# A third level buffer, later level steps, and six indexer dot products in flight with a projection's passes among them

## The chip, the cores and the metric

The kernel runs on one core of one Trainium2 chip. The metric is the device time of one execution in microseconds (us), lower is better. Before the change the median of three runs is 1547.05 us (1544.74 to 1548.55). The engines: TensorE (PE in the rows) multiplies matrices; PEld is its loading of weights; VectorE (DVE), ScalarE (ACT) and GpSimd (POOL) work elementwise; SyncE (SP) issues most transfers. Each engine runs its own list in order, and the lists meet at semaphores.

## The reference, cut to what matters

Two decoder layers, each of three parts: a mixer with three groups of heads, cross-attention into a fixed memory, and a mixture of gated experts. The change touches only the mixer:

```python
h = rms_norm(x, norm_mix[l]);  z = h @ w_in[l]          # 512 tokens, width 1024
# indexer: 8 heads of 64; every query keeps 128 causal keys
dots = einsum('bthd,bsd->bths', q_idx, k_idx) * 64**-0.5
score = einsum('bths,bth->bts', relu(dots), w_idx)       # causal mask, then top-k
# sparse attention: 6 heads of 64 on the kept keys, softmax, values
# gated linear attention (GLA): 4 heads, key width 48, value width 96
attn[t,s] = sum_d q[t,d] * k[s,d] * exp(b[t,d] - b[s,d]) # b = running sum of log decays
o = attn @ v + (q * exp(b)) @ state
# conformer branch: ca * sigmoid(cg), causal depthwise convolution with 31 taps, layer norm, silu
x = x + concat(o_gla, o_dsa, o_conv) @ w_out[l]
```

## The kernel before

Everything stays on one core, four tiles of 128 tokens. Projections that need full precision in the "split" form (`split_project`) run as three passes (head times head, rest times head, head times rest) per 128 rows of weights, so a projection of eight parts has 24 passes; the others (`project`) run one float32 product per part, which the trace shows as two records. A projection n goes into PSUM bank n % 2 and ScalarE evicts it (`evacuate`).

**Dot products.** After the index projections (`JOBS` "ik" and "iq") TensorE makes 32 dot products (`DOTS`: 4 tiles of tokens by 8 heads; 128, 256, 384, 512 columns wide), L806 to L811, each over 64 of the 128 rows, even heads in the upper half and odd ones in the lower. They go to the four banks 4 to 7. ScalarE takes the relu of each into one of four `relu` tiles (L1000 to L1005), VectorE weights and adds it to the scores `sel` (L1164 to L1172). A dot product waits for the relu four before it, a relu for the sum four before it. After the 32 dots comes the first query projection, `project(AFTER_IDX)` (L818), then five more projections of queries and keys with their norm sums, and four of values. Meanwhile VectorE does the top-k rounds (`selection`) and at the end six normalisations (L1193, semaphore `normed`), for which the first logits wait.

**Steps.** Then come 24 steps n = (tile i, head h) of attention. In each, TensorE turns the softmaxed row (`turn`, L843; it waits for `normalise(n)` on ScalarE, L1040), every second step makes the values of two heads (`values`, L854) and the logits of two more (`logits`, L834), and fills the rest with parts of other projections and GLA products, spread by a pace over `LAST_FILLED` = 22 steps (`work_of`, L534 to L547). On ScalarE a step is normalise(n), exps(n+1), the level's exponentials, `turned(n)` (eviction of the turned row), and at the end the evictions of the projections that ended in this step. On VectorE it is the reciprocal of the row sum (L1208), `masked(n+1)` (L1203), level work, top-k rounds of the last tile, convolution taps (`conv_tap`, L1217 to L1220; 62 of them, spread by `taps_spread` from the step after the gate "cg" is done up to step 21), and a level difference.

**Levels.** GLA's decayed products inside a tile are made in seven levels (`HALVES` 1 to 64). For level v: VectorE subtracts (`differences`, L1229), ScalarE takes exponentials (`level_decays`), VectorE multiplies the queries (`level_queries`, L1237), GpSimd the keys (`level_keys`, L1352), TensorE multiplies (`level_products`, L783), and VectorE or ScalarE merges the result into `AT`. Level v starts in step LEV0+v; the two `lev` buffers alternate, and a difference waits until the products two levels before are made. The product without decay (`diagonals`) uses buffer 1. By the pace before, LEV0 is 5, the gate's sigmoid runs in step 10 and the taps start in step 11.

The parts of `work_of` per step, before: 8, 8, 8, 7, 7, 5, 5, 4, 5, 5, 6, 6, 6, 6, 7, 7, 6, 6, 5, 4, 5, 3, 0, 0. The first four projections end exactly at the ends of steps 0, 1 and 2 and in step 4; heads 0 and 1 of GLA's output stand first in step 19, heads 2 and 3 end step 21.

## Time and profile before

| | |
|---|---|
| median of three runs | 1547.05 us (1544.74 to 1548.55) |
| profiled execution | 1550.28 us, of which 1548.4 us is the span of the trace |
| TensorE busy | 1435.3 us, 93% |
| VectorE busy | 1157.7 us, 75% |
| ScalarE busy | 908.0 us, 59% |
| GpSimd busy | 556.9 us, 36% |
| mean granted TensorE clock | 0.974 of full |
| dot products, layer 0 | 55.9 to 75.1 us |
| attention steps, layer 0 and 1 | 128.65 to 300.0 and 893.3 to 1064.6 us |

How to read it: times are us from the start of the span, unless marked ns. An instruction row gives start, length, engine, line of the kernel, operation and shapes; "x7" merges seven instructions in a row, and the square bracket is the idle time of the engine before it and what ended it. The granted clock is TensorE's, as a share of 2.4 GHz; 0.50 is its other level, 1.2 GHz.

### The profile page before, as it was taken

The page shows a single profiled execution, that of the slowest core. Times are in us where ns is not written, and L with a number is a line of the kernel's source. Part 1 is how long each engine was busy: PE and PEld are TensorE (multiplying, and loading weights), DVE is VectorE, ACT ScalarE, POOL GpSimd, SP SyncE. Part 2 cuts the span into 40 slices and gives each one's busy share as a digit, 9 for nine tenths or more (in the row PEclk, how much of TensorE's full clock was granted, in tenths as well). Part 3 has the DMA queues.
Part 4 walks back from the last instruction along what each step waited for, and adds up shares of the span by engine and source line. Part 5 has one row for each costly group of instructions (what it writes and reads, how often), then busy time and mean ns, then how long its engine had stood idle before and what let it go on. Part 6 is the DMA issues. An engine that isn't in the chain of part 4 may idle for free.

```text
span 1548.4 us, 20214 instructions
## 1 busy us (share of the span) xinstructions
PE 1435.3 (93%) x6710; PEld 1034.6 (67%) x6710; DVE 1157.7 (75%) x1658; ACT 908.0 (59%) x1346; POOL 556.9 (36%) x240
## 2 busy tenths in 40 slices
PE   7998989899899999999799989888988999999995
PEld 4686554557577888877556855544675778887773
DVE  4696579433469999999858955893334899999996
ACT  5643353553548787888475523546435587887881
POOL 2342332060004665553542413220600066555544
PEclk9999999999989999999999999999999899999998
DMA  6241601310428999999651421014131499999995
GB/s 222 92 109 41 216 1 55 137 57 11 153 109 288 397 398 399 398 398 399 232 190 42 109 75 74 1 55 144 49 107 57 154 342 399 399 399 398 398 397 177
DMA packets 151483, 312.72 MB, mean 202 GB/s; under 512 B 33158, under 2 KB 46380, under 8 KB 151228
## 3 DMA queue, kind: packets, MB, share of 16 engines
q1 hardware_dynamic: 140300, 271.39, 48.5%
q0 software_dynamic: 6624, 24.12, 4.2%
q10 hardware_dynamic: 4496, 16.40, 2.6%
q8 instruction: 36, 0.59, 0.2%
q14 instruction: 27, 0.22, 0.0%
HBM read 287.76 MB, written 29.50 MB: 205 GB/s over the span
## 4 chain that ended last, share of the span: by engine, by line
PE 50%; DVE 20%; DMA 15%; ACT 7%; issue 6%; POOL 1%; DVEq 1%; POOLq 0%; SPq 0%; ACTq 0%
PE ps L703 12%; DMA arena<-in_w_down 9%; PE ps L721 6%; DVE rest_w_down L1417 6%; PE ps L1494 4%; DMA arena<-in_w_gate 4%; DVE rest_w_up L1417 3%; DVE rest_w_gate L1417 3%; PE ps L1516 3%; DVE xg_rest L1430 2%; PE ps L724 2%; PE ps L810 2%; PE ps L1610 2%; PE ps L783 2%; ACT head_w_down L1412 1%
## 5 line engine op out<-in xcount | busy, mean ns | idle before, releaser
L2080 POOL TENSOR_TENSOR rest_w_down<-arena,head_w_down 128x2048 fp32r<-128x2048 f32 x30 | 191.3, 6377 | 191.5 <-ACT head_w_down L1412 191.5
L1417 DVE TENSOR_TENSOR rest_w_down<-arena,head_w_down 128x2048 fp32r<-128x2048 f32 x30 | 151.8, 5059 | 13.6 <-ACT head_w_down L1412 13.6
L1417 DVE TENSOR_TENSOR rest_w_gate<-arena,head_w_gate 128x2048 fp32r<-128x2048 f32 x64 | 145.8, 2279 | 0.1
L1417 DVE TENSOR_TENSOR rest_w_up<-arena,head_w_up 128x2048 fp32r<-128x2048 f32 x64 | 143.4, 2280 | 0.1
L1412 ACT ACTIVATE head_w_down<-arena 128x2048 fp32r<-128x2048 f32 x60 | 115.1, 1926 | 37.8 <-DMA arena<-in_w_down 37.4
L1412 ACT ACTIVATE head_w_gate<-arena 128x2048 fp32r<-128x2048 f32 x60 | 114.8, 1919 | 38.1 <-DMA arena<-in_w_gate 38.0
L1412 ACT ACTIVATE head_w_up<-arena 128x2048 fp32r<-128x2048 f32 x64 | 121.9, 1943 | 9.4 <-DMA arena<-in_w_up 9.4
L1401 PE MATMUL ps<-head_w_gate,xg_head 128*128 128x512 f32 x256 | 104.2, 407 | 4.4 <-DVE xg_rest L1430 3.5
L721 PE MATMUL ps<-hT,arena 128*128 128x512 f32 x224 | 106.4, 606 | 0.0
L1391 PE MATMUL ps<-head_w_down,he_head 128*128 128x512 f32 x240 | 99.6, 415 | 6.6 <-DVE rest_w_down L1417 4.1
L1403 PE MATMUL ps<-head_w_gate,xg_rest 128*128 128x512 f32 x256 | 100.2, 392 | 0.0
L1402 PE MATMUL ps<-rest_w_gate,xg_head 128*128 128x512 f32 x256 | 99.9, 390 | 0.0
L1401 PE MATMUL ps<-head_w_up,xg_head 128*128 128x512 f32 x256 | 99.8, 390 | 0.0
L1403 PE MATMUL ps<-head_w_up,xg_rest 128*128 128x512 f32 x256 | 99.7, 389 | 0.0
L1402 PE MATMUL ps<-rest_w_up,xg_head 128*128 128x512 f32 x256 | 99.6, 389 | 0.0
L1220 DVE SCALAR_TENSOR_TENSOR mixr<-arena,cf,mixr 128x512 f32<-128x512 f32 x120 | 94.4, 787 | 4.3
L1393 PE MATMUL ps<-head_w_down,he_rest 128*128 128x512 f32 x240 | 94.2, 392 | 0.0
L1392 PE MATMUL ps<-rest_w_down,he_head 128*128 128x512 f32 x240 | 93.6, 390 | 0.0
L2027 POOL DMA_INDIRECT xg<-hrows,slot_tok x2 | 4.9, 2437 | 240.8 <-DVE slot_tok L1998 240.8
L703 PE MATMUL ps<-hT_head,w_rest 128*128 128x512 f32 x224 | 89.0, 397 | 0.0
L2073 POOL DMA_INDIRECT xg<-hrows,idx x28 | 76.4, 2727 | 21.0 <-POOL idx L2086 21.0
L951 ACT ACTIVATE arena<-ps 128x512 f32<-128x512 f32 (+1 forms) x34 | 18.8, 558 | 110.0 <-PE ps L721 52.7
(366 smaller groups left out, 3545.4 us busy)
## 6 DMA issues: line engine op xcount, KB each, us to landing
arena<-in_w_gate SPq DMA_DIRECT2D x64, 1024.0 KB, 10.2
arena<-in_w_up SPq DMA_DIRECT2D x64, 1024.0 KB, 11.2
arena<-in_w_down SPq DMA_DIRECT2D x64, 1024.0 KB, 10.4
arena<-in_w_in SPq DMA_DIRECT2D x10, 1536.0 KB, 6.7
yrows<-yb ACTq DMA_DIRECT2D x30, 512.0 KB, 6.3
arena<-in_w_in SPq DMA_DIRECT2D x4, 2048.0 KB, 8.6
x<-in_x SPq DMA_DIRECT2D x8, 512.0 KB, 14.0
arena<-in_w_in SPq DMA_DIRECT2D x16, 256.0 KB, 4.9
```

Source lines behind the costliest of these rows:

```text
L703: last = nc.tensor.matmul(o, lhs, rhs, start=(c == 0 and a == 0), stop=(c == KD - 1 and a == 2))
L721: last = nc.tensor.matmul(ps[n % 2][0:width, :], w[:, c, col:col + width], hT[:, c, :], start=(c == 0), stop=(c == KD - 1))
L1220: do(nc.vector.scalar_tensor_tensor(o, cin[:, i, j:j + S], convw[:, i, j:j + 1], o, ALU.mult, ALU.add))
L1391: nc.tensor.matmul(out, ah, bh, start=(c == 0), stop=False)
L1392: nc.tensor.matmul(out, ah, bl, start=False, stop=False)
L1393: last = nc.tensor.matmul(out, al, bh, start=False, stop=(c == n - 1))
L1401: nc.tensor.matmul(ps[q][:, :], xh[:, c, :], wh[q][:, c, :], start=(c == 0), stop=False)
L1402: nc.tensor.matmul(ps[q][:, :], xh[:, c, :], wl[q][:, c, :], start=False, stop=False)
L1403: last = nc.tensor.matmul(ps[q][:, :], xl[:, c, :], wh[q][:, c, :], start=False, stop=(c == KD - 1))
L1412: nc.scalar.activation(wh[q][:, part(q, j), :], raw[q][:, part(q, j), :], ACT.Copy).then_inc(s_head[q], 1)
L1417: nc.vector.tensor_tensor(wl[q][:, c, :], raw[q][:, c, :], wh[q][:, c, :].bitcast(F32), ALU.subtract).then_inc(s_split[q], 1)
L2080: nc.gpsimd.tensor_tensor(wl[2][:, c, :], raw[2][:, c, :], wh[2][:, c, :].bitcast(F32), ALU.subtract)\
```

## The change

- The dots go to six banks (2 to 7) and six relu tiles (`RELUS`, `DOT_BANK`); the waits are on the relu and the sum six before.
- `project(AFTER_IDX)` after the dots is gone; its 24 passes are issued two at a time after every second dot from dot 9 on (`first_query_passes`).
- A third `lev` buffer, in the place of the second and third part of `gr`; `differences(v)` waits for the products three levels before; `level_queries(v)` comes a step later; the eviction of those parts of `gr` waits for all level products. `diagonals` uses the third buffer.
- ScalarE evicts the turned row before the level's exponentials.
- TensorE's order in a step: turn, logits, values, all parts, then diagonals and level products.
- The pace is set in two pieces: the projections of GLA's queries and keys and of the convolution over steps 0 to 7, the rest over steps 8 to 21. The parts per step become 10, 10, 9, 9, 7, 7, 6, 7, 5, 5, 5, 6, 4, 5, 6, 4, 6, 4, 4, 3, 5, 2, 0, 0. LEV0 becomes 4, the gate's sigmoid falls in step 7, the taps are spread from step 8 on (the first in step 10), heads 0 and 1 end step 18.

```diff
+RELUS = 6
-            lev = [view(mixg[:, :, :].rearrange("p h s -> p (h s)"), 1024 * i, 2, S) for i in range(2)]
+            lev = [view(mixg[:, :, :].rearrange("p h s -> p (h s)"), 1024 * i, 2, S) for i in range(2)] + [view(arena, up + 5120, 2, S)]
-            relu = view(scratch, 0, 4, S)
+            relu = view(scratch, 0, RELUS, S)
+            def DOT_BANK(n):
+                return 2 + n % RELUS
-            LAST_FILLED, FIRST_O = 22, 16
+            GATED, LAST_FILLED, FIRST_O = 8, 22, 16
+            def filler(names, steps):
+                return sum(LENGTH[JOBS[n][4]] for n, c in parts if JOBS[n][4] in names) + sum(attention(n) for n in steps)
-            total = sum(LENGTH[JOBS[n][4]] for n, c in parts) + sum(attention(n) for n in range(LAST_FILLED))
+            first, then = range(GATED), range(GATED, LAST_FILLED)
+            paces = [filler(("gq", "gk", "ca", "cg"), first) / len(first), filler(("gv", "kt", "gr", "upd", "o"), then) / len(then)]
-                pace += total / LAST_FILLED
+                pace += paces[n >= GATED]
+                def first_query_passes(start, end):
+                    if start == 0:
+                        pe.wait_ge(sN["proj_out"], AFTER_IDX - 1)
+                        pe.wait_ge(sN["heads_in"], 7)
+                        pe.wait_ge(sN["rests_in"], 4)
+                    wh, wl, at = w_head[0], w_rest[k_of(SPLIT[0])], slice(0, P)
+                    for m in range(start, end):
+                        c, a = m // 3, m % 3
+                        lhs, rhs = ((wh[:, c, at], hT_head[:, c, :]), (wl[:, c, at], hT_head[:, c, :]), (wh[:, c, at], hT_rest[:, c, :]))[a]
+                        last = nc.tensor.matmul(ps[AFTER_IDX % 2], lhs, rhs, start=(m == 0), stop=(m == 3 * KD - 1))
+                    if end == 3 * KD:
+                        last.then_inc(sN["proj_done"], 1)
                 for n, (i, h) in enumerate(DOTS):
-                    if n >= 4:
-                        pe.wait_ge(sN["relu_done"], n - 3)
+                    if n >= RELUS:
+                        pe.wait_ge(sN["relu_done"], n - RELUS + 1)
...
+                    if i and n % 2:
+                        at = n - IH - 1
+                        first_query_passes(at, at + 2)
-                project(AFTER_IDX)
...
                     turn(n)
+                    if n % 2 == 0 and n + 2 < NS:
+                        logits(n + 2)
+                        logits(n + 3)
                     if n % 2 == 0 and n:
                         values(n - 2)
-                    for job, c in work_of[n][:2]:
+                    for job, c in work_of[n]:
                         work(job, c)
...
-                    if n % 2 == 0 and n + 2 < NS:
-                        logits(n + 2)
-                        logits(n + 3)
-                    for job, c in work_of[n][2:]:
-                        work(job, c)
...
+                    if name == "gr" and i:
+                        act.wait_ge(sN["lev_mm"], NLEV + 1)
...
+                    turned(n)
                     if 0 <= n - LEV0 - 1 < NLEV:
                         level_decays(n - LEV0 - 1)
-                    turned(n)
...
-                    if v >= 1:
-                        dve.wait_ge(sN["lev_mm"], v)
+                    if v >= 2:
+                        dve.wait_ge(sN["lev_mm"], v - 1)
...
-                    if 0 <= n - LEV0 - 1 < NLEV:
-                        level_queries(n - LEV0 - 1)
+                    if 0 <= n - LEV0 - 2 < NLEV:
+                        level_queries(n - LEV0 - 2)
```

## Rows read from the trace of the kernel before

**Rows 1.** Sums of stretches: stretch, us, then each engine's busy us, clock, transfers.

```profile
56.80:75.10 18.30, 18.26 (x75) 11.34 (x76) 17.00 (x32) 15.51 (x32) 1.17 (x3) 1.00 0.24 84
...
191.70:288.30 96.60, 87.20 (x490) 50.33 (x490) 81.43 (x124) 45.87 (x97) 23.51 (x21) 0.98 0.06 23
...
956.40:1053.00 96.60, 87.19 (x490) 50.37 (x489) 81.42 (x125) 45.95 (x97) 23.88 (x21) 0.98 0.06 23
```

**Rows 2.** Waits of VectorE, 56.8 to 125.9: total us, times, longest.

```profile
DVE sel L1169 <- ACT scratch L1004: 6.8, 1, 6.8
```

**Rows 3.** Chain of waits, start of the first query projection.

```profile
70.92 11.13 PE ps L703 x48
```

**Rows 4.** Time line of VectorE: last dots added up, six normalisations.

```profile
69.61 5.47 DVE L1171 SCALAR_TENSOR_TENSOR sel<-scratch,iw,sel 128x512 f32<-128x512 f32 x7
...
120.97 4.67 DVE L1193 SCALAR_TENSOR_TENSOR scratch<-scratch,cf,ps 128x512 f32<-128x512 f32 x6
```

**Rows 5.** Time line of TensorE: first logits, first turned row.

```profile
126.47 0.49 PE L834 MATMUL ps<-scratch 64*128 64x128 f32 x4 [0.67 <-ACT scratch L951]
...
128.65 0.33 PE L843 MATMUL ps<-cf,scratch 128*128 128x128 f32 x1 [1.69 <-ACT scratch L1040]
```

**Rows 6.** Instructions by line and shape, both layers: dots of 512 columns.

```profile
L810 PE MATMUL ps<-sq,mixg 64*128 64x512 f32 x32 | 11.6, 641 | 0.0
```

**Rows 7.** Sums of two short stretches, for the granted clock.

```profile
130.00:132.00 2.00, 2.00 (x8) 1.04 (x6) 1.60 (x4) 0.00 (x0) 0.00 (x0) 0.50 0.88 323
...
270.00:272.00 2.00, 1.55 (x14) 1.55 (x15) 1.89 (x4) 1.70 (x4) 0.00 (x0) 1.00 0.00 0
```

**Rows 8.** Waits of TensorE, 128.6 to 288.3.

```profile
PE ps L843 <- ACT scratch L1040: 14.8, 12, 2.3
...
PE ps L783 <- ACT arena L1050: 0.7, 1, 0.7
...
PE ps L735 <- ACT arena L951: 0.3, 1, 0.3
```

**Rows 9.** Time line of TensorE: gaps before steps 1, 12, 19; half clock behind.

```profile
137.71 0.33 PE L843 MATMUL ps<-cf,scratch 128*128 128x128 f32 x1 [0.98 <-ACT scratch L1040]
...
216.76 0.55 PE L843 MATMUL ps<-cf,scratch 128*128 128x128 f32 x3 [2.35 <-ACT scratch L1040]
...
217.83 2.72 PE L724 MATMUL ps<-arena,hT 128*128 128x384 f32 x4
...
223.57 2.85 PE L724 MATMUL ps<-arena,hT 128*128 128x384 f32 x8
...
270.45 0.66 PE L843 MATMUL ps<-cf,scratch 128*128 128x128 f32 x4 [1.68 <-ACT scratch L1040]
```

**Rows 10.** Time line of ScalarE: table load for the sigmoid, copies of head 1.

```profile
203.43 1.28 ACT L954 ACT_TABLE_LOAD   x1
...
274.20 1.78 ACT L932 ACTIVATE mixg<-ps 32x512 f32<-32x512 f32 x3 [0.94 <-PE ps L758]
```

**Rows 11.** Waits of VectorE, 191.7 to 288.3.

```profile
DVE mixg L1229 <- PE ps L783: 4.8, 2, 2.9
...
DVE scratch L1203 <- PE ps L834: 4.2, 3, 2.5
```

**Rows 12.** Chain of waits at the end of the steps.

```profile
292.59 0.66 PE ps L843 x4
...
300.01 6.21 PE ps L903 x14
```

**Rows 13.** Time line of VectorE: difference, decays to the end, taps.

```profile
160.99 1.23 DVE L1229 TENSOR_TENSOR mixg<-arena 128x1024 f32<-128x1024 f32 x1
...
210.72 2.17 DVE L1258 TENSOR_TENSOR arena<-arena 128x1024 f32<-128x1024 f32 x1
...
239.32 5.48 DVE L1220 SCALAR_TENSOR_TENSOR mixr<-arena,cf,mixr 128x512 f32<-128x512 f32 x7
...
245.58 6.20 DVE L1220 SCALAR_TENSOR_TENSOR mixr<-arena,cf,mixr 128x512 f32<-128x512 f32 x7
```

More of the change, by code:

```diff
@@ L582, in vector_us @@
                 us += 1.5 if 0 <= n - LEV0 - 3 < BY_BLOCKS else 0.0
-                us += 0.8 if 0 <= n - LEV0 - 1 < NLEV else 0.0
+                us += 0.8 if 0 <= n - LEV0 - 2 < NLEV else 0.0
                 us += 1.3 if 0 <= n - LEV0 < NLEV else 0.0
@@ L766, in diagonals @@
                         for i in range(2):
-                            last = nc.tensor.matmul(ps[2][:, 4 * c + 2 * i:4 * c + 2 * i + 2], lev[1][:, i, P * c:P * c + P], gated,
+                            last = nc.tensor.matmul(ps[2][:, 4 * c + 2 * i:4 * c + 2 * i + 2], lev[2][:, i, P * c:P * c + P], gated,
                                                     start=True, stop=True)
@@ L1001, in _ @@
                     act.wait_ge(sN["dots_done"], n + 1)
-                    if n >= 4:
-                        act.wait_ge(sN["relu_used"], n - 3)
-                    nc.scalar.activation(relu[:, n % 4, 0:P * (i + 1)], ps[4 + n % 4][:, 0:P * (i + 1)], ACT.Relu,
+                    if n >= RELUS:
+                        act.wait_ge(sN["relu_used"], n - RELUS + 1)
+                    nc.scalar.activation(relu[:, n % RELUS, 0:P * (i + 1)], ps[DOT_BANK(n)][:, 0:P * (i + 1)], ACT.Relu,
                                          scale=ID ** -0.5).then_inc(sN["relu_done"], 1)
@@ L1069, in level_decays @@
                     act.wait_ge(sN["lev_d"], v + 1)
-                    d = halves(lev[v % 2], half)
+                    d = halves(lev[v % 3], half)
                     nc.scalar.activation(d[:, :, half:], d[:, :, half:], ACT.Exp)
@@ L1166, in _ @@
                     dve.wait_ge(sN["relu_done"], n + 1)
-                    r, w = relu[:, n % 4, 0:P * (i + 1)], iw[:, i, h:h + 1]
+                    r, w = relu[:, n % RELUS, 0:P * (i + 1)], iw[:, i, h:h + 1]
                     if h == 0:
@@ L1225, in differences @@
                         dve.wait_ge(sN["proj_out"], done("gk"))
-                    if v >= 1:
-                        dve.wait_ge(sN["lev_mm"], v)
+                    if v >= 2:
+                        dve.wait_ge(sN["lev_mm"], v - 1)
                     bv = halves(b, half)
-                    do(nc.vector.tensor_tensor(halves(lev[v % 2], half), bv, bv[:, :, half - 1:half].to_broadcast([P, 2 * S // (2 * half), 2 * half]),
+                    do(nc.vector.tensor_tensor(halves(lev[v % 3], half), bv, bv[:, :, half - 1:half].to_broadcast([P, 2 * S // (2 * half), 2 * half]),
                                                ALU.subtract), "lev_d")
@@ L1235, in level_queries @@
                     dve.wait_ge(sN["lev_e"], v + 1)
-                    d = halves(lev[v % 2], half)[:, :, half:]
+                    d = halves(lev[v % 3], half)[:, :, half:]
                     do(nc.vector.tensor_tensor(d, halves(gq, half)[:, :, half:], d, ALU.mult), "lev_q")
@@ L1350, in level_keys @@
                     gp.wait_ge(sN["lev_e"], v + 1)
-                    d = halves(lev[v % 2], half)[:, :, :half]
+                    d = halves(lev[v % 3], half)[:, :, :half]
                     do(nc.gpsimd.tensor_tensor(d, halves(gk, half)[:, :, :half], d, ALU.mult), "lev_k")
@@ L1367, in _ @@
                         do(nc.gpsimd.memset(AT, 0.0), "at_zero")
-                        do(nc.gpsimd.tensor_tensor(lev[1], gq, gk, ALU.mult), "lev_k")
+                        do(nc.gpsimd.tensor_tensor(lev[2], gq, gk, ALU.mult), "lev_k")
                     if 0 <= n - LEV0 - 3 < NLEV:
```

4 lines of the change are left out of this document (2 added, 2 removed).

## The prediction

> **What bounds the kernel now.** I read the sums of stretches first, then who waits for whom in them, then the time lines of single steps. A layer has two stretches that the change touches: the dot products of the indexer (56.8 to 75.1 us) with the top-k rounds and projections behind them, and the 24 attention steps (128.6 to 300 us). In the first, VectorE is the chain: 17.00 us of work in 18.30 [rows 1], and from 56.8 to 125.9 it waits for nothing after the first dot product [rows 2]. TensorE has slack there: its last dots end at 70.92 us and the first query projection (24 passes) stands behind them [rows 3], while VectorE adds up until 75.08 and, after all rounds, ends its six normalisations at 125.64 [rows 4]. TensorE starts the first logits at 126.47, 0.67 us after its last projection [rows 5]. In the steps TensorE is the longest engine, but not a full one: 87.20 of 96.60 us busy between 191.7 and 288.3; VectorE has 81.43 of the same 96.60. The second layer repeats this to 0.01 us [rows 1], so I work out one layer and double it.
>
> **Part 1, six dots in flight, the query passes among them.** Cost is order only: 32 dots, 24 passes as before. TensorE's work from dot 8 on is dots plus passes; two dots use different halves of the rows and overlap: eight dots of 512 columns are busy 5.8 us (11.6 for both layers [rows 6]), so a pair takes at most 1.45 us, and two passes 0.46 (48 in 11.13 us [rows 3]). VectorE takes 1.57 us for a pair (7 in 5.47 [rows 4]), so over 512 columns the two are nearly equal, and over 256 and 384 TensorE's two dots shrink with it. I take it that TensorE keeps up, with six products as cushion. It then ends the projection when the dots end, near 73 us in place of 76.4: 3.4 us earlier, and all projections up to 125.5 move up by as much. None of that reaches the steps: the first logits also wait for "normed" 6, which VectorE gives at 125.64 whatever TensorE does. So the gain is 126.47 less some 125.68, **0.8 us**. Bounds: 0.8 (nothing on VectorE gets shorter; its first dot waits for the same query eviction), and a loss if the passes break up the overlap: then a pair of 512 costs 1.7+0.46=2.2 against 1.57, for all three widths about 4 us late. The ScalarE and GpSimd work behind (the head of the next weights 2.8 us, its rest 6.8) shifts by under 1 us and has 3 us to the pass that needs it.
>
> The wait of TensorE before the steps grows from 0.67 to about 3.5 us. Today it is followed by half clock (1.2 GHz in place of 2.4: 0.50 at 130 to 132 us [rows 7]), in the new order too, perhaps a little sooner: no change, bounds -1 to +1 us.
>
> **Part 2, the steps.** TensorE's work stays the same to the instruction, so only its idle time and its clock count. Today, from 128.6 to 288.3, it idles 14.8 us for a normalised row of ScalarE, 0.7 for a level merge and 0.3 for an eviction [rows 8]: **15.8**. The kinds: (a) a projection ends exactly with the step, and its eviction (0.60) stands before the next normalise on ScalarE: 0.98 each in steps 1 to 3, 1.2 to 1.7 later; (b) VectorE's level difference waits for products of the same step, 1.46 before step 7; (c) step 12, 2.35 us: the sigmoid's table loads and VectorE's decays and first tap lie one behind the other [rows 9, 10]. After (c) four records of the value projection take 2.72 us where eight took 2.85: half clock, some 1.8 us with the products behind it. Together **17.6 us** that are no work.
>
> The new list: 9 to 10 parts a step up to step 3, so a projection now ends inside a step and later parts hide its eviction: (a) goes in steps 1 to 3. The third buffer and the extra step take (b) away. The gate is done in step 7, not 10, so (c) goes from step 12. But VectorE inherits: from level merge 1 on its list is today's list from 191.7 to 288.3, 81.43 us of work [rows 1] and some 3.4 of gaps between its 124 instructions (today it waits besides, 4.8 us for level products and 4.2 for logits [rows 11]). That is 84.8 us from the end of TensorE's step 7 to the last tap. TensorE's steps 8 to 21 hold 31 value parts of 0.70 us, 24 gate parts of 0.87, five level products of 2.0, 9.4 for key turns, updates and heads, and 18 for rows, logits and values: 80. **VectorE is longer by 5 us in this stretch**, where today TensorE is. By steps I find these waits of TensorE:
> - step 8: 0.9. Eviction 0.6, table 1.28 [rows 10], sigmoid 1.06, normalise 0.5 are 3.5 us; one part and a level product (2.65) hide the rest. Step 9: 0.3.
> - step 10: 2.1. VectorE's step 9 holds masked row 0.7, merges 1.5, queries 0.7, factors 4.1, difference 1.3, in all 8.3, against 5.7 plus what it was ahead.
> - steps 14 and 16: 0.5 and 2.6. VectorE 11 to 15, with 3, 5, 6, 7, 6 taps of 0.83: 30.5 us; TensorE 27.3.
> - step 18: 2.2. The state updates wait on VectorE for the last eviction, then 2.15 and 4 taps.
> - step 19: 3.4. Heads 0 and 1 now end step 18. Three copies (1.78, [rows 10]), a square 0.63 and the normalise 0.62 stand between, 3.1 at least; today gate parts come behind them and fill it.
> - step 21: 1.2, the third gate eviction ends with step 20, kind (a).
> These make 13.2; today's rows hold some 1.5 us of small waits (0.3 to 0.4) that such a walk doesn't see, and I add them: **14.7**. Ends: 11 if VectorE keeps its shorter tap, 19 if it has its longest.
>
> Clock: gaps of 2.35 and of 1.69 after 0.67 were followed by half clock [rows 5, 9], and so does the one before step 22, today and after; a single gap of 1.68 wasn't (1.00 at 270 to 272 [rows 7, 9]). Of the new gaps 2.6 and 3.4 are like the former, 2.1 and 2.2 between. At 1.8 us each, the one at 16 mostly hidden behind VectorE, I take **2.9** (0 to 5). The Trainium skill (TensorE: Matmul & The Clock Gate, section HAM oscillation) says that waits between groups of matmuls bring the slow clock back each time; the rows agree for the long gaps and not for 1.68.
>
> So the new idle is 14.7+2.9=17.6 against 17.6: the steps gain nothing. After step 21 both kernels are alike: the evictions of heads 2 and 3, 5.0 us to step 22 at 292.59, the end near 300 [rows 12]. The new wait on ScalarE (the second part of `gr` behind all level products) comes in step 17, the last product in step 12: nothing. Reordered logits cost nothing and spare VectorE the 4.2 us for which it waits on them [rows 11], which its list without waits already leaves out. The weight transfers behind are issued after semaphores of the same chain and move with it.
>
> **Sum.** 2 x 0.8 = 1.6 us faster. The profiled execution took 1550.28 us (span 1548.4 and 1.88 around it), 3.2 above the median of 1547.05; a difference carries over unchanged: **1545.5 us**, no change that a measurement can tell (about 0.3%, 4.6 us).
>
> **Rivals.** (1) The steps do gain. VectorE's taps run at 0.78 (7 in 5.48 [rows 13]), the gaps at 16 and 18 stay near 1 us and no half clock follows them: 3 us less idle and 2 of clock per layer, 10 in all, to 1536; half of it gives 1540. For it: VectorE waits 9.0 us in this list today, and all of kinds (a) to (c) do go. Against: the walk of VectorE has no slack from step 9 on. Chance 0.27.
> (2) Slower, by VectorE as the bound of steps 9 to 18. Taps collide with GpSimd: 7 in 6.20 us against 5.48, and a subtraction of the same size took 2.17 us beside GpSimd where it takes 1.23 alone [rows 13]. At 0.89 a tap the 61 taps cost 3.4 us more, nearly all on the path, and one more gap is followed by half clock, most of it hidden (1.0): 4.4 per layer, 1545.5+8.8=1554. It decides from about 2.5 us per layer, a tap of 0.87. Chance 0.2. The Trainium skill (SBUF — State Buffer, section Who interferes with whom) has it as a rule that a VectorE instruction with two inputs in SBUF and a GpSimd instruction that reads SBUF block each other; the 2.17 agrees. By it, the decays of step 8, which now fall in the time of the third level's keys, again take 2.2.
> (3) The dots fall behind, up to 4 us a layer on VectorE's chain: 1545.5+8=1553. Against: when TensorE is late, its dots are released together, and overlap best. Chance 0.05.
> (4) Forecast, within 0.3%: 0.48.
>
> Faster than by 0.3%: 0.27, same 0.48, slower 0.25. The range reaches from half of rival 1 and a little more, 1538, to rival 2, 1554.
>
> **What would show it.** Dots: first query passes between 60 and 73 us, first logits at 125.7, VectorE without waits before. If VectorE waits for the relus, rival 3. Steps: no 0.98 gaps in steps 1 to 3; the sigmoid near 190 in place of 203.43 us; a gap of 3 us after heads 0 and 1; the last tap ending 276 to 283 in place of 288.2; the phase's end (first ones-product of the head norms, today 300.01) within 2.5 us of 299.2. I would be wrong if the gaps at 10, 16 and 18 are missing (then rival 1), or if the first eight steps take longer than 64 us.

## The result, and the profile after

| | before | changed |
|---|---|---|
| median | 1545.89 us of 4 runs (1540.69 to 1548.55) | 1568.12 us of 4 runs (1564.87 to 1570.93) |
| ratio | | 1.0138, 95% interval 1.0108 to 1.0169 |
| profiled execution, span | 1550.28, 1548.4 us | 1564.87, 1562.8 us |
| VectorE busy, whole program | 1157.7 us | 1182.9 us |
| first dot to the steps' first transpose, each layer | 72.8, 72.6 us | 81.7, 81.7 us |
| first to last transpose of the 24 steps, each layer | 169.3, 169.3 us | 170.1, 170.2 us |
| first dot to the last product with the gate | 260.0, 259.8 us | 269.7, 269.9 us |

The change costs some 22 us, where 1.6 us of gain were forecast. In the traces the two mixers lose 19.8 us. The dots and the top-k behind them lose 9 us a layer, the steps 0.8. The two spans differ by only 14.4 us, since the rest of the program, which the change leaves alone, came out 5.4 us shorter in the changed kernel's profiled execution. Between the layers the rest takes 504.8 us before and 501.5 after, and 502.8 to 508.0 in six of the runs below. So a stage is compared by its own length here, and each such length comes from one profiled execution; the medians say what the whole program does.

The sums of two stretches of the changed kernel, which answer to [rows 1] (columns as there), and VectorE's waits between the dots and the normalisations, which answer to [rows 2]:

```profile
56.40:76.70 20.30, 19.79 (x83) 8.63 (x82) 16.99 (x32) 12.79 (x32) 1.01 (x3) 1.00 0.22 77
201.50:297.30 95.80, 82.74 (x482) 49.43 (x483) 83.65 (x131) 43.98 (x96) 23.86 (x22) 0.95 0.06 23
```

```profile
DVE sel L1194 <- ACT scratch L1029: 7.3, 2, 6.8
DVE sel L1196 <- ACT scratch L1029: 1.7, 6, 0.4
```

The 32 sums are again 17 us of work, but in 20.30 us and not 18.30: VectorE now waits for relus, 1.7 us in the six places of the second row and 0.5 us more in the first (7.3 less the 6.8 that it has before its first sum, as before). The rest of the loss stands in the time line. First VectorE and GpSimd before (start, length, engine, line, operation, idle time before it):

```profile
91.13 0.30 DVE L1180 TENSOR_SCALAR sel<-sel 128x256 f32<-128x256 f32 x1
...
92.43 6.82 POOL L1328 TENSOR_TENSOR w_rest<-arena,w_head 128x3072 fp32r<-128x3072 f32 x1 [9.95 <-ACT w_head L979]
...
111.48 0.36 DVE L1180 TENSOR_SCALAR sel<-sel 128x384 f32<-128x384 f32 x1
...
112.32 9.04 POOL L1328 TENSOR_TENSOR w_rest<-arena,w_head 128x4096 fp32r<-128x4096 f32 x1 [13.07 <-ACT w_head L979]
```

And after, with the normalisations, the first logits and the first transpose, which answer to [rows 4, 5]:

```profile
91.70 6.81 POOL L1353 TENSOR_TENSOR w_rest<-arena,w_head 128x3072 fp32r<-128x3072 f32 x1 [6.53 <-ACT w_head L1004]
...
92.72 5.93 DVE L1205 TENSOR_SCALAR sel<-sel 128x256 f32<-128x256 f32 x1
...
111.59 9.04 POOL L1353 TENSOR_TENSOR w_rest<-arena,w_head 128x4096 fp32r<-128x4096 f32 x1 [13.09 <-ACT w_head L1004]
...
118.71 2.15 DVE L1205 TENSOR_SCALAR sel<-sel 128x384 f32<-128x384 f32 x1
...
129.99 4.66 DVE L1218 SCALAR_TENSOR_TENSOR scratch<-scratch,cf,ps 128x512 f32<-128x512 f32 x6
...
134.71 0.80 PE L860 MATMUL ps<-scratch 64*128 64x128 f32 x4 [9.64 <-DVE scratch L1218]
137.22 0.48 PE L869 MATMUL ps<-cf,scratch 128*128 128x128 f32 x1 [1.72 <-ACT scratch L1065]
```

Line 1205 is the instruction that turns a finished selection into a mask, and line 1353 GpSimd's subtraction for the split weights. Before, each mask had begun 1.3 and 0.8 us ahead of the subtraction. Now, at the first of the two, VectorE is 1.6 us later and GpSimd 0.7 us earlier; both masks start inside the subtractions, and each ends 0.1 to 0.2 us after the subtraction does. They take 5.93 and 2.15 us where they took 0.30 and 0.36, **7.4 us a layer**. The MAX8 and MATCH_REPLACE of the same stretch keep their 0.43 and 0.41 us. With the 2.0 us of the sums that is 9.4 us on VectorE's chain, which sets the first logits: they come 0.06 us behind the last normalisation.

### The profile page after: what moved, and what is told of

It reads as the page before. It is cut to its first block, busy times and chain, and to the rows that moved or that the text cites. A ratio compares the mean times of both kernels' runs of the same rounds, so it can differ in the third digit from the quotient of the medians.

```text
span 1562.8 us, 20210 instructions
## 1 busy us (share of the span) xinstructions
PE 1433.9 (92%) x6710; PEld 1028.9 (66%) x6710; DVE 1182.9 (76%) x1658; ACT 907.1 (58%) x1346; POOL 555.7 (36%) x240
## 4 chain that ended last, share of the span: by engine, by line
PE 39%; DVE 33%; DMA 14%; issue 6%; ACT 6%; DVEq 1%; POOL 0%; SPq 0%; POOLq 0%; ACTq 0%
DMA arena<-in_w_down 10%; DVE rest_w_down L1442 7%; PE ps L713 6%; PE ps L731 6%; PE ps L1519 4%; DVE rest_w_up L1442 4%; DVE mixr L1245 3%; DVE sel L1203 3%; DVE m L1202 3%; PE ps L1541 3%; DVE rest_w_gate L1442 3%; DMA arena<-in_w_gate 2%; DVE xg_rest L1455 2%; PE ps L1635 2%; ACT head_w_down L1437 2%
## 5 line engine op out<-in xcount | busy, mean ns | idle before, releaser
L1245 DVE SCALAR_TENSOR_TENSOR mixr<-arena,cf,mixr 128x512 f32<-128x512 f32 x120 | 97.6, 813 | 4.3
L713 PE MATMUL ps<-hT_head,w_rest 128*128 128x512 f32 x208 | 83.3, 400 | 0.0
L1388 POOL TENSOR_TENSOR scratch<-sel,toep 128x256 f32<-128x256 f32 (+1 forms) x48 | 44.5, 928 | 107.9 <-DVE small L1228 105.8
```

What stands on the lines that cost most here:

```text
L713: last = nc.tensor.matmul(o, lhs, rhs, start=(c == 0 and a == 0), stop=(c == KD - 1 and a == 2))
L1245: do(nc.vector.scalar_tensor_tensor(o, cin[:, i, j:j + S], convw[:, i, j:j + 1], o, ALU.mult, ALU.add))
```

## The experiments

Ratios are against the kernel before on the same chip, with their 95% interval. A mask is the instruction that ends a tile's selection; the two that are given are those of tiles 1 and 2 in layer 0. "Logits" is the time from the first dot to the first logits (before 70.6 and 70.4, changed 79.2 and 79.2 us in the two layers). "Steps" is the time from the first to the last transpose. "Clock lost" is the sum of 1 less the granted clock over the steps, in us, from stretches of 2 us: 5.1 is about ten us at half clock. Logits, steps and clock lost are read from one profiled execution of each kernel, ratios from all of its runs.

**dots_only.** Part 1 of the change on the kernel before, nothing else.

```diff
+RELUS = 6
...
-                    nc.tensor.matmul(ps[4 + n % 4][:, 0:P * (i + 1)], iq[r, h // 2, P * i:P * i + P],
...
+                    nc.tensor.matmul(ps[DOT_BANK(n)][:, 0:P * (i + 1)], iq[r, h // 2, P * i:P * i + P],
...
+                    if i and n % 2:
+                        at = n - IH - 1
+                        first_query_passes(at, at + 2)
...
-                project(AFTER_IDX)
```

> The kernel before with the first part alone: six dots in flight and the first query projection's passes between them; every step of the 24 as before. My theory (the loss of about 21 us lies wholly between the dots and the first step): the dots end about 1.5 to 2 us late in each layer, the two finished-selection masks start inside GpSimd's long subtractions and take 5.9 and 2.2 us instead of 0.3 and 0.4, and the program is 17 to 22 us slower than before. The rival (the rebuilt steps, with their other order of TensorE's work, cost the time): within 3 us of before.

Measured: 1.0109 (1.0083 to 1.0136), 17.0 us slower. Logits 79.2 and 79.2, masks 5.92 and 2.13.

**steps_only.** The other part alone (against the changed kernel):

```diff
-RELUS = 6
+RELUS = 4
...
-                return 2 + n % RELUS
+                return 4 + n % RELUS
...
-                    if i and n % 2:
-                        at = n - IH - 1
-                        first_query_passes(at, at + 2)
...
+                project(AFTER_IDX)
```

> The changed kernel with its dots as before (four in flight, the first query projection behind them), and so the new order of the steps and the third level buffer alone. My theory: the dots end where they did, both masks end before GpSimd's subtractions start, and the steps themselves changed by under 1 us a layer: within 3 us of before. The rival (the steps cost the time): 15 to 22 us slower than before.

Measured: 0.9962 (0.9939 to 0.9986), 4.5 us faster, a little more than expected. Logits 70.5 and 70.4, steps 166.6 and 167.8 us. So the loss is that of the dots, and the steps alone are a gain, which neither theory had. From the first dot to the last product with the gate the traces of the two parts add up: dots_only is 22.8 us longer than before over both layers and steps_only 4.1 shorter, which makes 18.7 against the changed kernel's 19.8. The medians don't: 17.0 less 4.5 is 12.5 against 22. Each of the three has an interval of some 4 to 5 us to either side, and what is left of the difference stays open.

**after_rest_pieces.** The changed kernel, GpSimd's subtraction cut up:

```diff
-                    nc.gpsimd.tensor_tensor(w_rest[k][:, :, 0:w], chunk_at(SPLIT[m])[:, :, 0:w], w_head[m % 2][:, :, 0:w].bitcast(F32),
-                                            ALU.subtract).then_inc(sN["rests_in"], 1)
+                    for c in range(KD):
+                        last = nc.gpsimd.tensor_tensor(w_rest[k][:, c, 0:w], chunk_at(SPLIT[m])[:, c, 0:w], w_head[m % 2][:, c, 0:w].bitcast(F32),
+                                                       ALU.subtract)
+                    last.then_inc(sN["rests_in"], 1)
```

> The changed kernel, with GpSimd's subtraction for each later weight chunk issued as 8 pieces of 128x384 or 128x512 instead of one of 128x3072 or 128x4096. My theory (VectorE's mask instruction waits until the GpSimd instruction that was there first has ended): a mask waits for one piece, at most 1.2 us, and not for 5.6 us; 11 to 15 us faster than the changed kernel, 6 to 11 us slower than before, and the masks take 0.3 to 1.5 us. The rival (the masks are slow because both engines share bandwidth, whatever the size of an instruction): the masks stay at some 6 and 2 us, and the time is that of the changed kernel within 3 us.

Measured: 1.0039 (1.0021 to 1.0057), 4.8 us above before. The pieces, and the mask among them:

```profile
89.40 5.92 POOL L1354 TENSOR_TENSOR w_rest<-arena,w_head 128x384 fp32r<-128x384 f32 x6 [5.53 <-ACT w_head L1004]
...
90.42 1.11 DVE L1205 TENSOR_SCALAR sel<-sel 128x256 f32<-128x256 f32 x1
```

The masks take 1.11 and 0.47 us: they wait for one piece (1.02 us here), not for a share of the bandwidth. Logits 72.7.

**after_late_masks.** The changed kernel, the masks of tiles 1 and 2 behind the last round:

```diff
-                        if r == ROUNDS - 1:
+                        if r == ROUNDS - 1 and i == NT - 1:
...
+                for i in (1, 2):
+                    s = sel[:, i, 0:P * (i + 1)]
+                    do(nc.vector.tensor_scalar(s, s, 0.5 * (NEG + TAKEN), FAR, ALU.is_gt, ALU.mult), "sel_done")
```

> The changed kernel, with the two masks (tiles 1 and 2) moved behind the last MAX8 and MATCH_REPLACE rounds, where GpSimd has nothing left to subtract. My theory: both take 0.3 and 0.4 us there, 7.4 us a layer come back, 14 to 16 us faster than the changed kernel and 4 to 8 us slower than before (the rest is TensorE's slower pairs of dots). If the masks wait for something else than GpSimd's instruction (the rival: a delay that the changed order of the dots brings to VectorE itself), the lost time stays: within 3 us of the changed kernel.

Measured: 1.0007 (0.9982 to 1.0031), 3.0 us above before by the medians, which is within the noise; 0.29 and 0.36 us for the masks, logits 71.8 in both layers, 7.4 earlier than in the changed kernel. That is the 7.4 us, shown by taking away nothing but the coincidence. 1.2 us remain of the 2.0 of the sums, less the 0.8 that the logits gain.

**before_delay.** The kernel before, with VectorE made late:

```diff
+                        for _ in range(4 if i == 1 else 0):
+                            do(nc.vector.max(m8[:, :], s))
                         selection(i, range(ROUNDS_AHEAD if i == NT - 1 else ROUNDS))
```

> The kernel before, four dots in flight, with nothing changed but four more MAX8 on VectorE ahead of tile 1's selection (their result is overwritten; 0.43 us each, some 1.8 us in a layer). My theory (a delay of VectorE by more than 1.0 us is enough to let GpSimd's subtraction begin first): the mask of tile 1 takes about 5.9 us and that of tile 2 about 2 us, the first logits come 1.8 + 5.6 + 1.8 = some 9.2 us later in each layer, and the program is 14 to 20 us slower than before. The rival (the six banks or the passes cost the time): only the added 1.8 us a layer, 3 to 5 us slower.

Measured: 1.0104 (1.0067 to 1.0141), 17.8 us for 3.7 us of added work. The mask of tile 1 starts 0.57 us inside the subtraction:

```profile
92.11 6.81 POOL L1330 TENSOR_TENSOR w_rest<-arena,w_head 128x3072 fp32r<-128x3072 f32 x1 [9.93 <-ACT w_head L979]
...
92.68 6.39 DVE L1180 TENSOR_SCALAR sel<-sel 128x256 f32<-128x256 f32 x1
```

The second takes 2.14; logits 79.5 and 79.4. None of the change is in this kernel.

**six_only.** Six dots in flight over six banks, the projection whole behind them (against dots_only):

```diff
-                    if i and n % 2:
-                        at = n - IH - 1
-                        first_query_passes(at, at + 2)
...
+                project(AFTER_IDX)
```

> The kernel before with six dots in flight over six banks, and the first query projection whole behind them, as before. My theory (not the six banks but the passes between the dots make them TensorE's): the sums end 18.3 to 18.5 us after the first dot as before, the masks take 0.3 and 0.4 us, and the time is that of before within 3 us. The rival (the depth of six or its banks delays the sums): the sums end 20 us or more after the first dot, and the time is 15 to 20 us above before.

Measured: 1.0107 (1.0064 to 1.0150), 19 us. My theory fell by half. The last sum ends 19.2 and 19.1 us after the first dot in the two layers, as before, where it ends after 21.2 in the changed kernel. (The 18.3 to 18.5 us of the expectation are the time to the last sum's start.) So the 2.0 us are the passes' doing. But the masks wait all the same:

```profile
90.12 6.80 POOL L1334 TENSOR_TENSOR w_rest<-arena,w_head 128x3072 fp32r<-128x3072 f32 x1 [7.30 <-ACT w_head L985]
...
91.46 5.61 DVE L1186 TENSOR_SCALAR sel<-sel 128x256 f32<-128x256 f32 x1
```

Here VectorE is on time and GpSimd 2.3 us early: with six in flight the relus end sooner, and so do all of ScalarE's next tasks (the weight head at 87.28 and not 89.59 us). Either cause alone uses up the margin. Nobody gains by the early subtraction: TensorE runs without a wait from 86 to 126 us in this kernel and in the one before.

**after_mask_form.** The changed kernel, the mask as an instruction with two operands (column 61 of `small` holds FAR):

```diff
-                        if r == ROUNDS - 1:
+                        if r == ROUNDS - 1 and i < NT - 1:
+                            do(nc.vector.scalar_tensor_tensor(s, s, 0.5 * (NEG + TAKEN), small[:, 61:62].to_broadcast([P, P * (i + 1)]),
+                                                              ALU.is_gt, ALU.mult), "sel_done")
+                        elif r == ROUNDS - 1:
...
+                do(nc.vector.memset(small[:, 61:62], FAR))
```

> The changed kernel, with the masks of tiles 1 and 2 in the same place but as scalar_tensor_tensor with a constant read from a second operand, and not as tensor_scalar (the same numbers come out). If only the form with one tensor operand waits for GpSimd's instruction: the masks take 0.4 to 0.6 us where they took 5.9 and 2.2, and the kernel is 12 to 15 us faster than the changed one. If any VectorE instruction that starts there waits: 5.9 and 2.2 us again and the time of the changed kernel within 3 us.

Measured: 1.0113 (1.0074 to 1.0152), masks 5.92 and 2.21: this form waits too. It isn't "any instruction", since MAX8, which reads one tensor, and MATCH_REPLACE, whose eight values are loaded ahead, don't. Nor does a normalisation, whose second operand lies in PSUM: before the change one ran from 120.97 us beside the subtraction and took 0.75 us, as the five behind it did.

**after_warm.** The changed kernel, TensorE kept busy while it waits for the logits:

```diff
+                pe.wait_ge(sN["proj_out"], BEFORE_STEPS - 1)
+                for _ in range(13):
+                    nc.tensor.matmul(ps[BEFORE_STEPS % 2], ones[:, :], ones[:, 0:1].to_broadcast([P, 512]), start=True, stop=True)
                 pe.wait_ge(sN["normed"], 6)
```

> The changed kernel, with 13 products of ones on TensorE (0.59 us each, 7.7 us in all) in its wait of 9.6 us for the first logits; their result is overwritten. My theory (this wait lowers the granted clock to 0.50 for some 14 us, and the first steps lose what the new order of the steps gains): the clock stays near 1.00 up to the first step, the 24 steps take 166 to 168.5 us instead of 170.1, 3 to 7 us faster than the changed kernel. The rival (the first steps are set by VectorE and ScalarE, at either clock): within 2 us of the changed kernel.

Measured: 1.0159 (1.0108 to 1.0210). I had mis-sized it: a product leaves two records, and 13 took 11.4 us, so that the logits came 1.5 us behind the last normalisation. The clock stayed at 1.00 until 140 us, then fell to 0.50 for 3.4 us all the same. Steps 169.6 and 169.5, clock lost 8.5 where the changed kernel has 9.5. Inconclusive.

Then the parts of the steps, all with four dots in flight. **steps_late_logits** is steps_only with the logits behind two parts of the work and the level products again:

```diff
                     turn(n)
-                    if n % 2 == 0 and n + 2 < NS:
-                        logits(n + 2)
-                        logits(n + 3)
                     if n % 2 == 0 and n:
                         values(n - 2)
-                    for job, c in work_of[n]:
+                    for job, c in work_of[n][:2]:
                         work(job, c)
...
+                    if n % 2 == 0 and n + 2 < NS:
+                        logits(n + 2)
+                        logits(n + 3)
+                    for job, c in work_of[n][2:]:
+                        work(job, c)
```

**levels_only** has the old single pace besides, so that of the change there remain the third buffer and what is shifted with it; **levels_logits** is steps_only with this pace, and keeps the early logits:

```diff
-            first, then = range(GATED), range(GATED, LAST_FILLED)
-            paces = [filler(("gq", "gk", "ca", "cg"), first) / len(first), filler(("gv", "kt", "gr", "upd", "o"), then) / len(then)]
+            total = sum(LENGTH[JOBS[n][4]] for n, c in parts) + sum(attention(n) for n in range(LAST_FILLED))
...
-                pace += paces[n >= GATED]
+                pace += total / LAST_FILLED
```

> The kernel of steps_only (new steps, four dots in flight) with one part of the new steps undone: the next two logits again behind two pieces of the work and the level products, where they were before, and not right behind the transposes. At the same clock the new steps take 2.8 us a layer less than the old. If the earlier logits bring this: the steps take 169 us again, 5 us slower than steps_only. My theory: they bring about half of it, 167.5 to 168.5 us at 5.1 us of lost clock, 2 to 4 us slower than steps_only.

> The kernel before with the third level buffer alone (and with it the level queries one step later and the transposes' copy ahead of the level exponentials); the two paces and the early logits are undone as well. If the buffer and what is shifted with it bring the 2.8 us: steps of 166.5 to 167.5 us at 5.1 us of lost clock, 4 to 6 us faster than before. My theory: it brings under 1 us a layer, steps of 168.5 to 169.3 us, within 3 us of before.

> The kernel of levels_only (third level buffer, four dots in flight, the old pace of the work) with the early logits as well, and so without two parts of the change only: the six dots with passes, and the two paces. If the parts add up as the steps of the earlier runs say (at 5.1 us of lost clock: new steps 166.6, without the early logits 167.8, without the paces too 165.5 to 166.2): the steps take 164.3 to 165.0 us, 1 to 3 us faster than levels_only and 10 to 13 us faster than before. The rival (the early logits pay only with the two paces, whose work they go round): steps of 165.5 us or more, the time of levels_only within 2 us.

Measured, in this order: 1.0021 (0.9995 to 1.0048); 0.9961 (0.9938 to 0.9984); 0.9918 (0.9899 to 0.9937), which is 12.4 us faster than before. The steps of steps_late_logits came as expected, 167.8 us at 5.1 us of clock lost. Both expectations were too low for the old pace: levels_only gains 3.2 and 3.8 us a layer where I gave it under 1, and levels_logits 6.0 and 6.2.

**steps_warm, steps_fill, levels_fill.** Products of ones in TensorE's waits between the steps. The diff is steps_fill's, against steps_only; FILL gives their number behind each step, -1 ahead of the first. steps_warm, also on steps_only, has `{-1: 1, 10: 3, 16: 1, 18: 1, 19: 3, 21: 1, 22: 3}`, and levels_fill, on levels_logits, `{-1: 1, 11: 1, 18: 1, 19: 1, 21: 3}`:

```diff
+                FILL = {-1: 1, 9: 2, 15: 1, 17: 1, 18: 3, 20: 1, 21: 3}
+                def fill(n):
+                    if n >= 0:
+                        pe.wait_ge(sN["pt_out"], n + 1)
+                    for _ in range(FILL.get(n, 0)):
+                        nc.tensor.matmul(ps[6], ones[:, :], ones[:, 0:1].to_broadcast([P, 512]), start=True, stop=True)
...
+                fill(-1)
...
+                    if n in FILL:
+                        fill(n)
```

> The new order of the steps with four dots in flight (the kernel of steps_only), and products of ones in TensorE's waits: one before the first step (0.88 us; its wait is 1.7), three each behind steps 10, 19 and 22 (2.6 us; waits of 3.1, 3.7 and 3.5), one each behind steps 16, 18 and 21 (waits of 1.3 to 1.4); their result is overwritten. My theory (the granted clock falls behind such waits, and each us of clock lost costs the steps 0.85 us): the clock lost in the steps falls from 5.1 to 6.9 us to under 2, the 24 steps take 163.5 to 165.5 us instead of 166.6 and 167.8, and the kernel is 4 to 7 us faster than steps_only, some 10 us faster than before. The rival (what bounds the steps is VectorE and ScalarE, and the clock only goes along with it): steps of 166 us or more, the time of steps_only within 2 us.

> The kernel of steps_only with products of ones in TensorE's waits, this time where the waits are: one ahead of the first turned row (wait 1.7 us), two behind step 9 (3.1), one each behind steps 15 and 17 (1.4 and 1.4), three behind step 18 (3.7), one behind step 20 (1.3) and three behind step 21 (3.5); a product takes 0.9 to 1.0 us. Their result is overwritten. If the clock that falls behind long waits sets part of the steps' time: under 3 us of clock lost instead of 5.1 to 6.9, steps of 164 to 165.5 us, 2 to 5 us faster than steps_only. If it only goes along: steps of 166.6 us or more, no faster than steps_only, whatever the clock.

> The kernel of levels_logits with such products in its waits: one ahead of the first turned row (wait 1.7 us), one behind step 11 (2.1), one each behind steps 18 and 19 (1.7 and 1.4), three behind step 21 (3.5). If the clock sets part of the time: under 3 us of clock lost instead of 5.1, steps of 161 to 162.5 us instead of 163.3, 2 to 4 us faster than levels_logits and so the fastest kernel here. If not: steps of 163.3 us or more.

steps_warm: 1.0030 (1.0003 to 1.0056), steps of 175.0 and 173.7 us. I had put its products one step late, behind steps 10, 16, 18, 19, 21 and 22, while the waits lie ahead of those transposes. That is some 12 us of work (13 products of 0.9 us), and only three of the products, those ahead of step 0 and behind steps 18 and 21, stood in a wait. steps_fill: 0.9919 (0.9887 to 0.9951), against 0.9962 for steps_only. levels_fill: **0.9889** (0.9861 to 0.9917), 17.8 us faster than before and the fastest here; levels_logits has 0.9918. Each pair of intervals still overlaps, so that the gain of the filling rests on the lengths of the steps. What the steps took, by the clock lost in them:

| kernel | order of the steps | clock lost, layers 0, 1 | steps, us |
|---|---|---|---|
| before | old | 5.1, 5.1 | 169.3, 169.3 |
| before_delay | old | 9.4, 6.1 | 173.3, 169.8 |
| dots_only | old | 9.4, 6.2 | 173.4, 170.0 |
| six_only | old | 9.3, 6.1 | 173.2, 169.8 |
| changed | new | 9.5, 9.5 | 170.1, 170.2 |
| after_late_masks | new | 9.9, 9.7 | 170.7, 170.4 |
| after_rest_pieces | new | 9.9, 5.7 | 170.7, 166.9 |
| after_mask_form | new | 9.8, 9.6 | 170.7, 170.3 |
| after_warm | new | 8.5, 8.5 | 169.6, 169.5 |
| steps_only | new | 5.1, 6.8 | 166.6, 167.8 |
| steps_warm | new, filled one step late | 8.5, 6.8 | 175.0, 173.7 |
| steps_fill | new, filled | 1.7, 3.4 | 163.5, 163.6 |
| steps_late_logits | new, late logits | 6.8, 5.1 | 169.6, 167.8 |
| levels_only | old, third buffer | 5.1, 5.1 | 166.1, 165.5 |
| levels_logits | old, third buffer, early logits | 5.1, 5.1 | 163.3, 163.1 |
| levels_fill | the same, filled | 1.7, 0.0 | 161.3, 159.7 |

The sums over the steps of layer 0 show where the time goes (the first number behind the stretch is its length, then come the busy us of TensorE, its weight loads, VectorE, ScalarE and GpSimd, and the granted clock). Here are before, changed, and levels_fill up to 0.8 us before its last transpose.

```profile
128.70:298.00 169.30, 151.60 (x798) 90.85 (x798) 115.62 (x197) 68.47 (x155) 39.16 (x35) 0.97 0.24 87
```

```profile
137.20:307.30 170.10, 152.73 (x798) 93.77 (x798) 119.87 (x197) 69.62 (x155) 39.44 (x35) 0.94 0.22 79
```

```profile
128.70:289.50 160.80, 151.05 (x805) 91.49 (x806) 115.03 (x198) 69.49 (x156) 37.83 (x35) 0.99 0.24 85
```

And levels_only, levels_logits and steps_only, whose clock is that of the kernel before:

```profile
128.10:294.30 166.20, 151.19 (x798) 91.09 (x798) 113.78 (x197) 69.16 (x155) 36.21 (x35) 0.97 0.25 88
```

```profile
128.80:292.10 163.30, 149.34 (x798) 92.31 (x798) 115.25 (x197) 68.91 (x155) 38.42 (x35) 0.97 0.25 90
```

```profile
128.70:295.30 166.60, 149.25 (x798) 92.41 (x798) 119.81 (x197) 69.52 (x155) 39.41 (x35) 0.97 0.24 88
```

Two things follow. First, a us of clock lost costs the steps 0.6 to 1 us, and it is a cause: only TensorE's idle time was filled, with work of no use, and the steps became shorter. From levels_logits to levels_fill they lose 2.0 us for 3.4 of clock, and 3.4 for 5.1; from steps_only to steps_fill 3.1 for 3.4, and 4.2 for 3.4, of which at least 0.8 must be something else, since a stretch at half speed loses at most half of its length.

Second, at the same 5.1 us the parts of the new order have these prices: the third buffer -3.2 to -3.8 us, the early logits -2.4 to -2.9 with the old pace (-1.2 with the new, across the two layers), and the two paces **+3.4** (163.2 to 166.6, layer 0). With the late logits the paces cost 2.3 (165.5 to 167.8, layer 1). The medians agree: levels_logits and steps_only are 0.0044 apart, 3.4 us a layer. The sums tell the kinds apart. The third buffer takes 2.7 us of idle time off TensorE (17.7 before, 15.0 in levels_only). The early logits take 1.0 off its idle time and 1.9 off its busy time, with the same 798 records. The paces leave its busy time alone and add 3.4 us of idle time (14.0 to 17.4). The paces' price has a mark on VectorE, too. Its level differences, before, changed, and with the old pace (levels_logits), by line in the steps:

```profile
L1229 DVE TENSOR_TENSOR mixg<-arena 128x1024 f32<-128x1024 f32 x7 | 9.0, 1284 | 10.2 <-PE ps L783 8.1 <-PE ps L767 2.0
```

```profile
L1254 DVE TENSOR_TENSOR mixg<-arena 128x1024 f32<-128x1024 f32 x5 | 9.6, 1911 | 0.2
L1254 DVE TENSOR_TENSOR arena<-arena 128x1024 f32<-128x1024 f32 x2 | 3.6, 1810 | 0.1
```

```profile
L1247 DVE TENSOR_TENSOR mixg<-arena 128x1024 f32<-128x1024 f32 x5 | 6.2, 1238 | 1.7 <-ACT arena L969 1.5
L1247 DVE TENSOR_TENSOR arena<-arena 128x1024 f32<-128x1024 f32 x2 | 2.9, 1427 | 0.1
```

The seven take 13.2 us in the changed kernel, 9.0 and 9.1 in the others; one that started at 187.38 inside GpSimd's 187.11 to 188.70 took 2.40 us. It is the masks' wait again, in small. The last tile's mask, too, takes 1.38 us in steps_only and 0.43 in levels_logits. In steps_late_logits the seven differences take 10.6 us, for a price of 2.3. That VectorE's longer instructions are the whole of the 3.4 is argued, not shown.

## Why the prediction was wrong, point by point

- **The first logits wait for "normed" 6, "which VectorE gives at 125.64 whatever TensorE does".** This step failed. VectorE's own work was taken as fixed from the dots on; it grew by 7.4 us a layer, since it met GpSimd's subtractions. I had asked of ScalarE's and GpSimd's work only who needs its result ("shifts by under 1 us and has 3 us to the pass that needs it"): the shift was 0.7 us, and right. What it was moved into was not asked. Before the change the two engines missed each other by 1.0 and 0.5 us (end of the mask to start of the subtraction), which the time line showed.
- **"I take it that TensorE keeps up, with six products as cushion."** This step failed too: TensorE's time for a pair of dots with its two passes was mis-sized. Over 512 columns it is 1.72 us, against VectorE's 1.57. My own terms, 1.45 and 0.46, already come to 1.91, and the forecast took an overlap of the two for granted. The changed kernel's time line:

```profile
68.12 1.13 PE L834 MATMUL ps<-sq,mixg 64*128 64x512 f32 x4
69.18 0.50 PE L806 MATMUL ps<-hT_head,w_rest 128*128 128x512 f32 x1
69.52 0.40 PE L806 MATMUL ps<-hT_rest,w_head 128*128 128x512 f32 x1
69.84 1.13 PE L834 MATMUL ps<-sq,mixg 64*128 64x512 f32 x4
```

  From pair to pair are 1.72 us, of which two passes between two pairs take 0.66. That "over 256 and 384 TensorE's two dots shrink with it" was true of the dots and not of the passes: from pair to pair are 1.30 and 1.51 us there, against VectorE's 1.04 and 1.31. So VectorE was the faster at all three widths. The cushion covered the 256 columns; 1.3 us were lost by the first sum over 512, and 0.7 over 512. The sums ended 2.0 us late: rival 3 (up to 4 us, a chance of 0.05) had the mechanism and this sign, and nothing behind it. By the mechanism alone it would have been 4 us for both layers in place of its 8; with the collision behind it, 19.
- **The gain of 0.8 us at the first logits**: right. They wait for nothing but the normalisations, 0.06 us.
- **TensorE's wait of 3.5 us before the steps, "no change" in the clock.** The wait became 9.64 us, for VectorE's delay, and the half clock behind it lasted to 142 us, 5.3 us into the steps. In layer 0 of steps_only it lasts to 4.3 us into them and begins behind the first transpose. The first step took 10.0 us where steps_only has 9.2: 0.8 us.
- **The new gaps of TensorE.** Forecast 0.9, 2.1, 0.5, 2.6, 2.2, 3.4 and 1.2 us ahead of steps 8, 10, 14, 16, 18, 19 and 21; measured 0.88, 3.08, 1.19, 1.42, 1.38, 3.67 and 1.30. The 0.98 of steps 1 to 3 are gone, and the sigmoid's table load starts at 198.79, 61.6 us into the steps (forecast near 190, 61 us into them). The last tap ends 156.1 us into them (159.6 before), where 147 to 154 was forecast. The waits, to be read with [rows 8]:

```profile
PE ps L869 <- ACT scratch L1065: 15.2, 9, 3.7
PE ps L745 <- ACT arena L976: 0.3, 1, 0.3
```

```profile
217.21 0.44 PE L869 MATMUL ps<-cf,scratch 128*128 128x128 f32 x2 [3.08 <-ACT scratch L1065]
```

```profile
280.57 1.12 PE L869 MATMUL ps<-cf,scratch 128*128 128x128 f32 x4 [3.67 <-ACT scratch L1065]
281.48 4.47 PE L731 MATMUL ps<-hT,arena 128*128 128x512 f32 x5
```

  15.5 us against a forecast of 14.7, with 15.8 before, and the steps at +0.8 us a layer against 0. The closeness is luck in part, for the sum has two wrong terms that cancel. "TensorE's work stays the same to the instruction, so only its idle time and its clock count" missed that the same instructions take less time in the new order: in steps_only its busy time falls from 151.60 to 149.25 us at equal clock, and the steps from 169.3 to 166.6. Against it stand the 3.5 us by which the changed kernel's steps are longer than those of steps_only, for 4.3 us more clock lost: 0.8 in the first step, and 2.6 behind the 3.67 before step 19. There the clock was at 0.50 for 6.8 us in both layers of the changed kernel, while in layer 0 of steps_only it stayed at 1.00 behind the same wait (3.66). Why, no run here shows. The sign "the first eight steps take longer than 64 us" came true by 0.4 us (64.4 in both layers, 63.6 and 62.0 in steps_only), with the late start in it. Half clock came behind the gaps of 3.08 and 3.67 (five projection records take 4.47 us there), not behind that of 1.42 which I had at 2.6. My walk did have VectorE as the bound of steps 9 to 18, and rival 2 the collision with GpSimd, but laid on the taps. It sat on the level differences; a tap is 0.81 us in steps_only and levels_logits alike.
- **The Trainium skill** (SBUF — State Buffer, section Who interferes with whom) says that a VectorE instruction with two SBUF inputs, and a tensor_scalar too where it enters a 2-port mode, contends with GpSimd for a shared port pair, and that whichever came first blocks the other until it is done. The 5.93 and 6.39 us of tensor_scalar, the 5.92 of the two-input form and the 0.43 of MAX8 beside the same subtraction agree with it; in all of them GpSimd came first, and they say nothing of the other order. I had applied it to taps and decays, for part 2, and not to part 1.

The range ended at 1554 because no case had the collision behind the late sums: a chance for "something on VectorE meets GpSimd between dots and logits" was not given at all.

## What to carry to other kernels

When a change shifts an engine's work by even 1 us, go down the time lines of VectorE and GpSimd side by side, and note for each short VectorE instruction how far it is from a long GpSimd one: a margin of 0.5 us here was worth 7 us a layer, and a delay of VectorE by 1.8 us made the logits 9 us later. Keep the long one in pieces (1 us of wait at most, and GpSimd is done 1 us later), or the short one out of its time. Try the parts of a change singly: here the third buffer (with the orders that come with it) and the early logits alone are 0.8% faster, and the rest of the change, the six dots with their passes and the two paces, costs more than that.

## What the runs showed of the hardware

- A mask of 0.30 us took 5.61 to 6.39 us when it started within GpSimd's 6.8 us, and ended 0.1 to 0.2 us after it; MAX8 and MATCH_REPLACE beside the same instruction kept 0.43 and 0.41 us.
- GpSimd's subtraction takes 1.02 us for each 128x384 piece. The records of neighbours overlap a little, and eight end 7.9 us after the first starts, against 6.82 in one (after_rest_pieces, changed).
- The granted clock mostly fell to 0.50 behind waits of TensorE of 2 to 4 us within otherwise full work, though not behind the 3.66 in layer 0 of steps_only. With the waits filled by products of ones it stayed at 1.00 over a whole layer's steps (levels_fill, layer 1); the steps were 3.4 us shorter for it. Products placed where there was no wait cost 6 to 8 us a layer (steps_warm). In layer 0 of levels_fill it fell at 181.6 us for 3.4 us, where TensorE's only waits from 165 us on were of 0.42 and 0.36 us. So a long wait isn't the only thing that lowers it, and what decides between two alike places these runs don't settle.
- A product of ones (fp32, 128x512) leaves two records and takes 0.9 to 1.0 us, not the 0.59 of one record.
